# Three slots' low parts on GpSimd, and 4 products of zeros in place of 12

## The chip, the cores and the metric

The kernel runs on one core of one Trainium2 chip. The metric is the device time of one execution in microseconds, the median of three timed runs. One more execution was recorded by the hardware profiler, and all rows shown below are of that execution. TensorE is PE in the rows, VectorE is DVE, ScalarE is ACT, GpSimd is POOL and SyncE is SP.

## The reference

Two transformer blocks over 256 tokens of width 1024, all in float32. The first has two layers: latent attention (MLA), then sliding-window attention (SWA), each followed by an MLP of width 4096. The second has three branches (an RWKV recurrence, stick-breaking attention, attention to 256 memory tokens), gates over them and a convolutional feed-forward. Around the change the reference does this:

```
x = _layernorm(alpha * x + swa, ln_mix_g, ln_mix_b)      # third norm, "ln2" in the kernel
h = relu(x @ w_up); y = (h * h) @ w_down                  # "mlp1"
x = _layernorm(alpha * x + y, ln_mlp_g, ln_mlp_b)         # fourth norm, "ln3"
p = rms_norm(x, norm1_g) @ w_in                           # fifth norm, "rms1", then "rwkv"
...
kv = rms_norm(mem, mem_g) @ w_kv                          # "memka" and "memkb" make its keys
```

## The kernel before

**Products in three parts.** Each float32 operand is cut into a high part (rounded to the format fp32r) and a low part (the rest). A product is three matmuls: high by high, low by high, high by low.

**Weights in slots.** All weights come as one stream of slots of 128x1024 values (512 KB), in the order of the list STREAM, through a ring of four buffers (RING = 4). SP loads a slot into `raw`. ACT makes its high part `whi` (L1435) and raises the semaphore `cut_hi`. DVE then subtracts (`wlo` = `raw` - `whi`, L2047) and raises `cut_lo`. PE waits on `cut_lo` before it reads a slot. SP waits on `cut_lo` too: it loads slot n once the low part of slot n-4 is made. ACT makes the high part of slot n once PE has begun slot n-3. The call `cuts(stage, s)` on ACT and on DVE makes slot `SLOT[stage] + s + 3` (AHEAD = 3), so it stands some steps ahead of the slot's use. Where each call stands is written by hand in the program of each engine.

**The three slots of this change.** Slot A is the second of `mlp1`; its cut comes at the last share of the attention's output product. Slot B is the third of `memkb`; its cut comes behind the last hidden unit of `mlp1`. Slot C is the first of `rwkv`; its cut comes between the fourth norm and the fifth.

**Norms.** `residual` (L2070) is four DVE instructions over a quarter of the tokens' values each (128x512). A quarter waits for its accumulator bank `acc` to be full, reads the bank from PSUM and `x` from SBUF, and writes `res` and a sum. ACT squares each quarter (L1500), DVE works out mean and variance in small instructions (L2074 to L2089), ACT takes the root (L1505). For `ln2` DVE and ACT scale the quarters (L2097, L1516), PE transposes them (L764, in `feature_major`), ACT makes the high parts `xh` and DVE the low parts `xl`, and `chunk_pair` begins the next product. Ahead of `ln2` PE computes the chunk `memka`, ahead of `rms1` the three chunks `memkb` and then products of zeros. Between `ln3` and `rms1` DVE makes `x` in eight instructions (L2354, then L2359, each 128x512, each reading two tensors in SBUF), ACT squares it again, and DVE scales it (L2117). In `chunk_pair` PE waits for the low part of the second of two slots before its first product.

**GpSimd** does a few memsets and DMA issues, in program order. Ahead of the place of the change it issues the bias rows of `swa`, behind it the rows of the fourth norm's gain and bias (`affine_rows(3)`), which wait for DVE late in `mlp1`, and then two memsets that wait for the fifth norm's root.

Of the kernel before, what the change touches and what calls it, by code (L numbers as in the profile page):

```python
# [17 lines left out]
F32 = mybir.dt.float32  # L18
# [3 lines left out]
ALU = mybir.AluOpType  # L22
# [5 lines left out]
DC = D // P  # L28
# [5 lines left out]
FC = DFF // P  # L34
# [5 lines left out]
RING = 4  # L40
AHEAD = 3
# [5 lines left out]
SLOT = {}  # L47
# [120 lines left out]
SWA_SLOT = {key: n for n, key in enumerate(SWA_SLOTS)}  # L168
# [140 lines left out]
def build(nc, w, xt, x_tok, ln_rows, memt, mem_tok, consts_in, band_in, params_in, lora_in, gate2_in, relb_in, out):  # L309
    ctx = ExitStack()  # L310
    with ctx:
# [8 lines left out]
        raw = tensor(ctx, "raw", [P, RING, 1024])  # L320
        whi = tensor(ctx, "whi", [P, RING, 1024], F32R)
        wlo = tensor(ctx, "wlo", [P, RING, 1024], F32R)
# [130 lines left out]
        def of_tokens(name, width=2):  # L453
            first = {"mem_sum": 0, "mem_square": 2, "inverse": 4, "root": 8, "q_root": 10, "less_q_root": 12, "mem_least": 14, "large": 16, "rms_eps": 17, "lnx_eps": 18}[name]
            return cols[:, first:first + width]
# [98 lines left out]
        cut_hi = sem("cut_hi")  # L554
        cut_lo = sem("cut_lo")
# [3 lines left out]
        def sig(name):  # L559
            if name not in named:  # L560
                named[name] = sem(name)
            return named[name]
# [48 lines left out]
        @block.gpsimd  # L611
        def _(pool):
            nc.gpsimd.memset(zeros[:, :], 0.0).then_inc(sig("zeros_set"), 1)

            def affine_rows(n):

                if n:
                    pool.wait_ge(sig("affine_done"), n)
                else:
                    wait_drained(pool, ("mla", ("o", MLA_H - 1)))  # L620
                pool.dma_start(gb[:, :, :].rearrange("p a d -> p (a d)"), bass.AP(ln_rows.tensor, n * 2 * D, [[0, P], [1, 2 * D]]))\
                    .then_inc(sig("affine_loaded"), 16)

            nc.gpsimd.memset(of_tokens("large", 1), 3.0e38).then_inc(sig("large_set"), 1)
            nc.gpsimd.memset(of_tokens("rms_eps", 1), RMS_EPS).then_inc(sig("eps_set"), 1)
            nc.gpsimd.memset(of_tokens("lnx_eps", 1), LNX_EPS).then_inc(sig("eps_set"), 1)
            pool.dma_start(relb[:, :], relb_in).then_inc(sig("band_loaded"), 16)
            pool.dma_start(bandt, band_in).then_inc(sig("band_loaded"), 16)

            wait_drained(pool, ("brow", 0))  # L630
            pool.dma_start(scratch, brow).then_inc(sig("brow_stored"), 16)
            pool.wait_ge(sig("brow_stored"), 16)
            pool.dma_start(lora[:, :], lora_in).then_inc(sig("lora_loaded"), 16)
            pool.dma_start(gate2[:, :], gate2_in).then_inc(sig("lora_loaded"), 16)
            pool.wait_ge(sig("qr_ready"), 2)
            pool.dma_start(con[:, CCOL["blockones"]:], consts_in[:, CCOL["blockones"]:]).then_inc(sig("con2_loaded"), 16)

            def bias_rows(head, heads, loaded):


                pool.dma_start(bias[:, head % 8:head % 8 + heads, :], bass.AP(scratch.tensor, head * 384, [[1, P], [384, heads], [1, T]]))\
                    .then_inc(sig(loaded), 16)

            affine_rows(0)
            bias_rows(0, 8, "bias_loaded0")
            affine_rows(1)
            affine_rows(2)
            for first in (8, 12):
                for n in range(first - 8, first - 4):
                    wait_drained(pool, ("swa", ("s", n)))  # L650
                for half_ in (0, 4):
                    bias_rows(8 + (first - 8) // 2 + half_, 2, f"bias_loaded{first}")
            affine_rows(3)

            pool.wait_ge(sig("rstd"), 5)
            for j in range(3):
                wait_drained(pool, ("memkb", j))
            nc.gpsimd.memset(pb[:, :, 0:1], 0.0).then_inc(sig("pb_zero"), 1)
            nc.gpsimd.memset(cum[:, :, 0:1], 0.0).then_inc(sig("pb_zero"), 1)
            wait_drained(pool, ("mem", ("o", 3)))  # L660
            nc.gpsimd.memset(cg[:, :, 0:2], 0.0).then_inc(sig("cg_zero"), 1)
            nc.gpsimd.memset(cv[:, :, 0:2], 0.0).then_inc(sig("cg_zero"), 1)
# [3 lines left out]
        def _(pe):  # L666
# [85 lines left out]
            def feature_major(name, idle=0):  # L752


                n = SCALED[name]
                zero_products(open_result((name, 0)), idle)
                for d, t in ((0, 0), (0, 1), (1, 0), (1, 1)):
                    if (d, t) == (1, 0):
                        pe.wait_ge(sig("scaled_act"), n + 1)
                    else:  # L760
                        pe.wait_ge(sig("scaled_dve"), 3 * n + d + t + 1)
                    for i in ((0, 1, 2), (3, 4))[d]:
                        for c, dst in turned_chunks(name, i):
                            last = nc.tensor.transpose(dst[:, half(t)], rest[:, t, c * P:c * P + P], C("ident"))  # L764
                        if t == 1 and i < 4:
                            last.then_inc(sig("turned"), 1)
                        elif t == 1:
                            close_result(last, (name, 0))
# [104 lines left out]
            for p in range(4):  # L873
                bank = open_result(("k", p))
                for e in range(2):
                    for c in range(2):
                        s, tile = divmod(2 * (2 * p + e) + c, 8)
# [14 lines left out]
            for kind, n in MLA_PE:  # L892
# [10 lines left out]
                elif kind in "rn":  # L903
                    bank = open_result(key)
                    for e in range(2):
                        for k in range(3):
                            s, tile = divmod(MLA_TILE[(kind, n)] + 3 * e + k, 8)
# [127 lines left out]
            mlp("mlp1", "ln2")  # L1035
            for j in range(3):
                chunk("memkb", j, ("memkb", j), memh, meml)
            feature_major("rms1", 12)
            chunk_pair("rwkv", [("rwkv", 0), ("rwkv", 1)], "rms1")
            for j in range(2, 4):  # L1040
                chunk("rwkv", j, ("rwkv", j), xh, xl)
# [132 lines left out]
            for tc in range(2):  # L1174
# [98 lines left out]
                for c in range(4):  # L1273
                    for src, of in ((vtok[:, tc, :], rk), (sa, rb)):
                        for g, off in enumerate(HALVES):
                            h = 2 * c + g
# [98 lines left out]
            for r in range(24):  # L1375

                bank = open_result(("branch", r))
                n = SLOT["branch"] + r // 2
# [659 lines left out]
        def _(dve):  # L2038
# [10 lines left out]
            def cuts(stage, s, it=None, per=0):  # L2049
                cut(SLOT[stage] + s + AHEAD, it, per)  # L2050

            def fill_cut(i):

                cuts("sbqk", i)
# [59 lines left out]
            def rms_norm(name, g, ahead=None):  # L2114
                inverse(name, False)
                for t, d in ((0, 0), (1, 0), (1, 1)):
                    ts(tok(rest, t, d), tok(x, t, d), column("rstd", t), None, ALU.mult).then_inc(sig("scaled_dve"), 1)  # L2117
                if ahead:
                    ahead()
                for i in range(5):  # L2120
                    dve.wait_ge(sig("x_hi"), 5 * SCALED[name] + i + 1)
                    for c, src in turned_chunks(name, i):
                        ins = stt(xl[:, c, :], src, G(g, c), xh[:, c, :].bitcast(F32), ALU.mult, ALU.subtract)
                    if i < 4:
                        ins.then_inc(sig("x_low"), 1)
                    else:
                        drain(ins, (name, 0))
# [199 lines left out]
            for p, turn in enumerate(SWA_TURNS):  # L2327
                heads = (2 * p, 2 * p + 1) if p < 8 else ()
                if p in (0, 4, 6):
                    dve.wait_ge(sig(f"bias_loaded{2 * p}"), 32 if p else 16)  # L2330
                for h in heads:
                    g = SWA_ORDER[h]
                    negative_scores("swa", h, three, SWA_D ** -0.5, (bias[:, g % 8, P - 1::-1], bias[:, g % 8, ::-1]), nsink[:, g:g + 1])
                for kind, h in turn:
                    if kind == "q":
                        cuts("swaqo", SWA_SLOT[(kind, h)])
                for h in heads:
                    normalise("swa", h, three, True)
                for kind, h in shares_last(turn):
                    if kind == "o":  # L2340
                        key = ("swa", ("o", h))
                        dve.wait_ge(sig("oh_hi"), 8 + h + 1)
                        drain(minus(ol[:, h, :], work[RESULT[key] % 4][:, 0:T], oh[:, h, :]), key)
                    elif kind == "w":
                        cuts("swaqo", SWA_SLOT[(kind, h)])
            layer_norm("ln2", "swa", "ln_mix_g", "ln_mix_b", 8)
            cuts("memka", 0)
            mlp("mlp1", FC, 2)
            cuts("mlp1", 2 * FC - 1)
            residual("ln3", "mlp1")  # L2350
            dve.wait_ge(sig("affine_loaded"), 64)
            for t in range(2):
# [4 lines left out]
            for t in range(2):  # L2357
                for d in range(2):
                    stt(tok(x, t, d), tok(x, t, d), column("rstd", t), tok(gb, 1, d), ALU.mult, ALU.add).then_inc(sig("x_made"), 1)  # L2359
            cuts("memkb", 0)  # L2360
            rms_norm("rms1", "norm1", lambda: cuts("memkb", 1))
            cuts("memkb", 2)
            dve.wait_ge(sig("pb_zero"), 2)
            def by_halves(tile):
# [497 lines left out]
```

## Time and profile before

| | |
|---|---|
| median of 3 runs | 1086.45 us (1086.35 to 1087.44) |
| profiled execution | 1088.7 us, of which the span of its instructions is 1086.9 us |
| granted TensorE clock, mean | 0.998 |
| PE busy | 1065.5 us (98%) |
| DVE busy | 762.2 us (70%) |
| ACT busy | 642.5 us (59%) |
| POOL busy | 10.0 us (1%), 27 instructions |
| third norm | about 378 to 391 us from the span's start |
| fourth and fifth norm | about 566 to 586 us |

Busy shares are averages over the whole span. PE's records overlap, so a busy PE says little; what counts at a norm is where PE's next product waits. In a timeline each row gives the start, the duration, engine, line and operation, what is written and read, a count, and in brackets how long the engine had been idle before it and who released it. Where a row merges several instructions, its duration is that of the whole group.

### The profile page before, as it was taken

The numbers are of one execution on the slowest core, as the hardware profiler recorded it, in microseconds if no ns is written. First come the engines' busy times: TensorE is split into PE (matmuls) and PEld (weight loads), VectorE is DVE, ScalarE is ACT, GpSimd is POOL, SyncE is SP. The second block draws the span as 40 slices with busy tenths as digits, with TensorE's granted clock in tenths as the row PEclk, the third lists the DMA queues.
The fourth block names the chain that finished last, engine by engine and source line by source line (L and its number), as shares of the span: only waits on it lengthen the run. The fifth ranks groups of instructions, "written<-read, shape, count | busy, mean of one in ns | idle before, by whom it ended". The sixth has DMA issues, their size and how long they took to land.

```text
span 1086.9 us, 22249 instructions
## 1 busy us (share of the span) xinstructions
PE 1065.5 (98%) x8247; PEld 960.5 (88%) x8247; DVE 762.2 (70%) x1313; ACT 642.5 (59%) x1159; POOL 10.0 (1%) x27
## 2 busy tenths in 40 slices
PE   6999999999999999999999999999999999999998
PEld 5978999988887789988988988898899979999997
DVE  4877756557796775555677878646774968777776
ACT  4876654544676764444558874435567448666663
POOL 1000000000000000000000000000000000000000
PEclk9999999999999999999999999999999999999999
DMA  9545565566665346666663533122245655656562
GB/s 350 181 164 203 190 189 191 185 184 183 204 211 156 103 154 191 187 182 186 181 230 119 165 126 115 44 79 79 78 156 173 195 155 160 206 177 185 186 193 94
DMA packets 49170, 181.76 MB, mean 167 GB/s; under 512 B 5536, under 2 KB 5696, under 8 KB 48208
## 3 DMA queue, kind: packets, MB, share of 16 engines
q1 hardware_dynamic: 46512, 168.32, 49.1%
q0 software_dynamic: 1584, 7.63, 2.4%
q10 hardware_dynamic: 1008, 4.89, 1.2%
q8 instruction: 47, 0.77, 0.3%
q14 instruction: 19, 0.16, 0.0%
HBM read 179.74 MB, written 1.07 MB: 166 GB/s over the span
## 4 chain that ended last, share of the span: by engine, by line
PE 91%; DVE 4%; ACT 3%; issue 1%; DMA 1%; POOL 0%; DVEq 0%; ACTq 0%; POOLq 0%
PE acc L739 28%; PE work L686 13%; PE work L690 13%; PE work L689 13%; PE acc L686 4%; PE acc L689 3%; PE acc L690 3%; ACT whi L1435 1%; DVE wlo L2047 1%; PE work L724 1%; DMA qlat<-band_rows 1%; DVE res L2070 1%; PE work L810 1%; PE work L887 1%; PE work L714 1%
## 5 line engine op out<-in xcount | busy, mean ns | idle before, releaser
L2047 DVE TENSOR_TENSOR wlo<-raw,whi 128x1024 fp32r<-128x1024 f32 x319 | 388.9, 1223 | 143.5 <-ACT whi L1435 141.8
L1435 ACT ACTIVATE whi<-raw 128x1024 fp32r<-128x1024 f32 x319 | 335.9, 1056 | 120.2 <-PE acc L739 84.2
L686 PE MATMUL work<-xh,whi 128*128 128x256 f32 x1024 | 290.2, 283 | 0.6 <-ACT k_ L1776 0.2
L689 PE MATMUL work<-xl,whi 128*128 128x256 f32 x1024 | 289.2, 282 | 0.0
L690 PE MATMUL work<-xh,wlo 128*128 128x256 f32 x1024 | 289.1, 282 | 0.0
L686 PEld LDWEIGHTS work<-xh,whi 128*128 128x128 f32 x1024 | 194.5, 190 | 7.9 <-issue 2.1
L689 PEld LDWEIGHTS work<-xl,whi 128*128 128x128 f32 x1024 | 194.2, 190 | 3.5
L690 PEld LDWEIGHTS work<-xh,wlo 128*128 128x128 f32 x1024 | 194.8, 190 | 0.0
L739 PE MATMUL acc<-whi,hl 128*128 128x512 f32 x344 | 108.0, 395 | 0.0
L739 PE MATMUL acc<-wlo,hh 128*128 128x512 f32 x344 | 108.0, 395 | 0.0
L739 PE MATMUL acc<-whi,hh 128*128 128x512 f32 x344 | 108.0, 395 | 0.0
L686 PE MATMUL acc<-xh,whi 128*128 128x256 f32 x288 | 86.8, 301 | 0.0
L1669 ACT ACTIVATE ha<-work 128x256 f32<-128x256 f32 x64 | 24.6, 384 | 99.7 <-PE work L686 94.8
L689 PE MATMUL acc<-xl,whi 128*128 128x256 f32 x288 | 81.3, 282 | 0.0
L690 PE MATMUL acc<-xh,wlo 128*128 128x256 f32 x288 | 81.3, 282 | 0.0
L739 PEld LDWEIGHTS acc<-whi,hl 128*128 128x128 f32 x344 | 64.5, 188 | 15.8
L739 PEld LDWEIGHTS acc<-wlo,hh 128*128 128x128 f32 x344 | 64.5, 187 | 15.4
L739 PEld LDWEIGHTS acc<-whi,hh 128*128 128x128 f32 x344 | 59.5, 189 | 8.4
L2288 DVE TENSOR_TENSOR hb<-ha 128x256 f32<-128x256 f32 x64 | 27.2, 425 | 45.4 <-ACT ha L1669 45.4
L686 PEld LDWEIGHTS acc<-xh,whi 128*128 128x128 f32 x288 | 54.8, 190 | 3.3 <-issue 1.4
L689 PEld LDWEIGHTS acc<-xl,whi 128*128 128x128 f32 x288 | 54.9, 191 | 0.8 <-issue 0.7
L690 PEld LDWEIGHTS acc<-xh,wlo 128*128 128x128 f32 x288 | 54.8, 190 | 0.0
(456 smaller groups left out, 1635.5 us busy)
## 6 DMA issues: line engine op xcount, KB each, us to landing
raw<-weights SPq DMA_DIRECT2D x319, 512.0 KB, 3.6
gb<-ln_rows POOLq DMA_DIRECT2D x4, 1024.0 KB, 7.4
memraw<-mem_t ACTq DMA_DIRECT2D x1, 1024.0 KB, 15.4
x<-mem_tok ACTq DMA_DIRECT2D x1, 1024.0 KB, 18.5
x<-x_tok ACTq DMA_DIRECT2D x1, 1024.0 KB, 7.8
qlat<-bias_scratch POOLq DMA_DIRECT2D x1, 1024.0 KB, 9.8
qlat<-bias_scratch POOLq DMA_DIRECT2D x4, 256.0 KB, 4.2
out_tok<-res SPq DMA_DIRECT2D x4, 256.0 KB, 2.1
```

Of the source, the lines that this page charges most:

```text
L686: a = mm(dst, whi[:, n % RING, col], hi, start=start, stop=False, skip_group_check=shared)
L689: mm(dst, whi[:, n % RING, col], lo, start=False, stop=False, skip_group_check=shared)
L690: return mm(dst, wlo[:, n % RING, col], hi, start=False, stop=stop, skip_group_check=shared)
L714: a = mm(banks[j][:, 0:T], whi[:, (n + j) % RING, col], xh[:, k, :], start=k == 0, stop=False)
L724: last = mm(banks[j][:, 0:T], whi[:, (n + j) % RING, k * P:k * P + P], xl[:, k, :], start=False, stop=k == DC - 1)
L739: ins = mm(acc[2 * t + d][:, :], left[:, half(t)], right[:, n % RING, d * 512:d * 512 + 512], start=first and a == 0, stop=last and a == 2)
L810: last = mm(dst, src[:, half(t)], one.broadcast_to([P, heads, width // heads]), start=True, stop=True)
L887: last = nc.tensor.transpose(bank[:, b * P:b * P + P], probability_buffer(stage, h)[:, a * P:a * P + P], C("ident"))
L1435: act_fn(whi[:, n % RING, :], raw[:, n % RING, :], ACT.Copy).then_inc(cut_hi, 1)
L1669: act_fn(ha[:, f % 2, :], bank[:, 0:T], ACT.Relu).then_inc(sig("relu"), 1)
L2047: tt(wlo[:, n % RING, :], raw[:, n % RING, :], whi[:, n % RING, :].bitcast(F32), ALU.subtract).then_inc(cut_lo, 1)
L2288: tt(hb[:, f % 2, :], ha[:, f % 2, :], ha[:, f % 2, :], ALU.mult).then_inc(sig("h_squared"), 1)
```

## The change

Three low parts are no longer made by DVE but by GpSimd, with the same subtraction, in GpSimd's own program order. GpSimd waits for the slot before to have its low part and for the slot's own high part. DVE waits for GpSimd ahead of the slots that follow A and C, so that the counts of `cut_lo` stay in order. The products of zeros ahead of the fifth norm's transposes go from 12 to 4.

```diff
+            def low_part(n):
+
+                pool.wait_ge(cut_lo, n)
+                pool.wait_ge(cut_hi, n + 1)
+                nc.gpsimd.tensor_tensor(wlo[:, n % RING, :], raw[:, n % RING, :], whi[:, n % RING, :].bitcast(F32), ALU.subtract).then_inc(cut_lo, 1)
+
...
+            low_part(SLOT["swaqo"] + SWA_SLOT[("w", DC - 1)] + AHEAD)
             affine_rows(3)
+            low_part(SLOT["mlp1"] + 2 * FC - 1 + AHEAD)
+            low_part(SLOT["memkb"] + AHEAD)
...
-            feature_major("rms1", 12)
+            feature_major("rms1", 4)
...
+            def cuts_behind_pool(stage, s):
+
+                dve.wait_ge(cut_lo, SLOT[stage] + s + AHEAD)
+                cuts(stage, s)
+
...
-                    elif kind == "w":
+                    elif kind == "w" and h < DC - 1:
                         cuts("swaqo", SWA_SLOT[(kind, h)])
             layer_norm("ln2", "swa", "ln_mix_g", "ln_mix_b", 8)
-            cuts("memka", 0)
+            cuts_behind_pool("memka", 0)
             mlp("mlp1", FC, 2)
-            cuts("mlp1", 2 * FC - 1)
             residual("ln3", "mlp1")
...
-            cuts("memkb", 0)
-            rms_norm("rms1", "norm1", lambda: cuts("memkb", 1))
+            rms_norm("rms1", "norm1", lambda: cuts_behind_pool("memkb", 1))
             cuts("memkb", 2)
```

## Rows read from the trace of the kernel before

**Rows 1.** The page: shares of the chain that ended last, by engine.
```profile
PE 91%; DVE 4%; ACT 3%; issue 1%; DMA 1%; POOL 0%; DVEq 0%; ACTq 0%; POOLq 0%
```

**Rows 2.** Timelines of DVE, third norm: slot A's cut, first and last quarter, variance.
```profile
376.87 1.22 DVE L2047 TENSOR_TENSOR wlo<-raw,whi 128x1024 fp32r<-128x1024 f32 x1 [0.30 <-ACT whi L1435]
378.01 0.68 DVE L2070 SCALAR_TENSOR_TENSOR res<-x,acc 128x512 f32<-128x512 f32 x1
...
379.83 0.68 DVE L2070 SCALAR_TENSOR_TENSOR res<-x,acc 128x512 f32<-128x512 f32 x1
...
381.46 0.16 DVE L2088 TENSOR_TENSOR stat<-stat 128x2 f32<-128x2 f32 x1
```

**Rows 3.** Timeline of PE, third norm: last banks, transposes.
```profile
377.62 0.63 PE L739 MATMUL acc<-whi,ol 128*128 128x512 f32 x2
...
382.86 1.28 PE L764 MATMUL acc<-con,res 128*128 128x128 f32 x10 [1.77 <-DVE res L2097]
```

**Rows 4.** Timelines of PE and DVE ahead of the sixth norm, where DVE is not late.
```profile
889.42 0.63 PE L739 MATMUL acc<-whi,xl 128*128 128x512 f32 x2
...
889.85 2.69 DVE L2676 TENSOR_TENSOR x<-x,acc 128x512 f32<-128x512 f32 x4 [1.36 <-PE acc L739]
```

**Rows 5.** Timelines of ACT, third norm: table load, first and last square.
```profile
376.86 1.28 ACT L1485 ACT_TABLE_LOAD   x1
...
378.80 0.63 ACT L1500 ACTIVATE sqr<-res 128x512 f32<-128x512 f32 x1 [0.44 <-DVE res L2070]
...
380.65 0.61 ACT L1500 ACTIVATE sqr<-res 128x512 f32<-128x512 f32 x1
```

**Rows 6.** Timeline of DVE, fourth and fifth norm.
```profile
565.40 1.22 DVE L2047 TENSOR_TENSOR wlo<-raw,whi 128x1024 fp32r<-128x1024 f32 x1 [0.91 <-ACT whi L1435]
...
568.37 0.68 DVE L2070 SCALAR_TENSOR_TENSOR res<-x,acc 128x512 f32<-128x512 f32 x1
...
569.69 2.74 DVE L2354 SCALAR_TENSOR_TENSOR x<-res,stat,gb 128x512 f32<-128x512 f32 x4
...
575.94 1.22 DVE L2047 TENSOR_TENSOR wlo<-raw,whi 128x1024 fp32r<-128x1024 f32 x1
...
577.28 0.16 DVE L2088 TENSOR_TENSOR stat<-stat 128x2 f32<-128x2 f32 x1
...
579.10 1.22 DVE L2047 TENSOR_TENSOR wlo<-raw,whi 128x1024 fp32r<-128x1024 f32 x1
```

**Rows 7.** Timeline of ACT, fourth and fifth norm: two high parts, last square.
```profile
569.74 1.99 ACT L1435 ACTIVATE whi<-raw 128x1024 fp32r<-128x1024 f32 x2
...
576.06 0.63 ACT L1500 ACTIVATE sqr<-x 128x512 f32<-128x512 f32 x1
```

**Rows 8.** Timeline of PE, fourth and fifth norm.
```profile
566.15 0.63 PE L739 MATMUL acc<-whi,hl 128*128 128x512 f32 x2
566.62 0.28 PE L686 MATMUL work<-memh,whi 128*128 128x256 f32 x1
...
575.14 2.76 PE L750 MATMUL work<-zeros 128*128 128x512 bf16 x12
578.45 1.31 PE L764 MATMUL acc<-con,res 128*128 128x128 f32 x10 [0.55 <-DVE res L2117]
...
580.58 0.36 PE L714 MATMUL work<-xh,whi 128*128 128x256 f32 x1 [0.16 <-issue]
```

**Rows 9.** Timeline of POOL, whole span: two memsets.
```profile
0.74 0.20 POOL L613 MEMSET zeros<- 128x128 bf16 x1 [0.29 <-POOLq L2856]
...
579.35 0.11 POOL L659 MEMSET cum<- 128x8 f32 x1
```

**Rows 10.** The page: DMA issues of `raw` (count, size, median us to landing).
```profile
raw<-weights SPq DMA_DIRECT2D x319, 512.0 KB, 3.6
```

**Rows 11.** Timeline of PE at the start: first and last of 26 products.
```profile
10.19 1.46 PE L861 MATMUL work<-qlat,relb 32*16 32x384 f32 x2 [10.19 <-DMA qlat<-band_rows]
...
11.96 0.41 PE L689 MATMUL work<-xl,whi 128*128 128x256 f32 x1
...
17.29 0.41 PE L690 MATMUL work<-xh,wlo 128*128 128x256 f32 x1
```

## The prediction, made before the change was built

> **What bounds the kernel now.** I read the page's chain of work that ended last, then the waits of PE, then the timelines of each engine at the three norms. The chain runs through PE for 91% of the span [rows 1], so a microsecond taken off another engine counts only where PE waits for that engine. At the third norm the wait is plain: PE has idled 1.77 us when the transposes start at 382.86, released by DVE's scaling [rows 3]. At the fifth norm PE idles 0.55 us ahead of the transposes at 578.45, and it stood in 2.76 us of products of zeros just before [rows 8]; so for 578.45 - 575.14 = 3.3 us it had nothing of use to do. Before both waits DVE makes a low part of 1.22 us in the middle of the norm's chain: slot A at 376.87 [rows 2], slot B at 565.40 and slot C at 575.94 [rows 6]. The question is what each stands in front of.
>
> **Third norm, slot A.** Without the cut a quarter of the residual starts when its bank is full. How soon that can be is read ahead of the sixth norm: the last pair of matmuls of a half starts at 889.42 and DVE at 889.85, 0.43 us later [rows 4]. Here the second half's last pair starts at 377.62 [rows 3], so its quarters (the third and fourth) can start at 378.05 and, with the pitch of (379.83 - 378.01) / 3 = 0.61 us, at 378.66. The fourth started at 379.83 [rows 2]: DVE is 1.17 us earlier. But ACT is in between. It loads a function table at 376.86 for 1.28 us, and the first square at 378.80 shows an idle time of only 0.44 us [rows 5]: ACT is free at 378.36 whatever DVE does. Its squares have a pitch of (380.65 - 378.80) / 3 = 0.62 us, so the last one moves from 380.65 to 380.21. From the last square the chain is serial (variance, root, scaling, transposes). I take **0.40 us** of gain, 0.44 less a little for the step out of the table load. DVE's remaining 0.7 us goes into waiting for ACT.
>
> **Fourth norm, slot B.** The last pair starts at 566.15 [rows 8], so the fourth quarter can start at 566.15 + 0.43 + 0.61 = 567.19. It started at 568.37 [rows 6]: **1.18 us**. ACT is no limit: its squares follow, and its two high parts (569.74 [rows 7]) end more than 1 us before the root is wanted. The second of them needs PE to be in the second `memkb` chunk. The three chunks fill 566.62 to 575.14 [rows 8], 2.84 us each, so that is from 569.46 on, and it costs nothing. After the small instructions the eight two-tensor instructions that make `x` follow back to back, so all 1.18 us is kept.
>
> **Slot C.** The cut ran from 575.94, and the next thing DVE did on the chain was the variance at 577.28 [rows 6]. Without the cut this instruction waits for ACT's last square, which started at 576.06 [rows 7]. At the third norm it came 381.46 - 380.65 = 0.81 us after the last square [rows 2, 5], here that makes 576.87, a gain of **0.41 us**. The rest of the 1.22 us goes to the wait for ACT.
>
> **Zeros.** With 1.59 us gained, transposes can start at 578.45 - 1.59 = 576.86. Twelve products of zeros take 2.76 us and would end at 577.90, so they would have eaten 1.0 us of that. Four end at 575.14 + 4 x 0.23 = 576.06 and leave PE idle for 0.8 us. That part costs nothing and gains nothing beyond letting the 1.59 us through. What sets PE's first real product at 580.58 is the low part of the slot after C, at 579.10 for 1.22 us [rows 6, 8]; it hangs on the same DVE chain and moves with it.
>
> **What GpSimd's subtraction costs.** No row has one. From below: memsets take 0.11 us for 8 columns and 0.20 for 128 [rows 9], some 0.8 ns a column, so 1024 columns written once would be 0.9 us. From above, with two streams read and one written, each at that pace: 0.1 + 3 x 0.8 = 2.6 us. I take 2.6, since the subtraction does have three streams. The Trainium skill ("GPSIMD Engine Reference", section "Elementwise — side-by-side cycle accounting") gives 4497 ns for 2048 values of a two-input float32 instruction, which would be an estimate of 2.25 us here. No run here shows it.
>
> Slack, in times of before: A can start when ACT's high part is done, at about 376.9, and PE needs it only behind transposes that start at about 382.4, 5.5 us later. B starts at 565.45 and is wanted by PE's third `memkb` chunk at 575.14 - 2.84 = 572.3. C starts behind its high part, about 1.2 us earlier than 569.74 + 1.0, at 569.5, and is wanted by DVE at about 577.5. All three bear some 5 us. SP loads the slot four further on behind each low part: behind A and B those loads go out about 1.5 us later, behind C some 4 us earlier. A load lands in 3.6 us [rows 10] and its cut is three slots of PE work later, so none becomes late. Behind A, GpSimd's next entry is a DMA wanted near the end of `mlp1`; behind C come two memsets that wait for the fifth root in any case. DVE's two new waits are over before DVE gets there.
>
> **Sum.** 0.40 + 1.18 + 0.41 = 1.99, call it 2.0 us. The profiled execution would go from 1088.7 (span 1086.9) to 1086.7 (1084.9). It lay 2.25 us above the median of the runs, 1086.45; so the forecast for the median is **1084.4 us**, 0.19% less. The measurement can tell about 0.2% (2.2 us) from no change. The gain lies just inside that.
>
> **Rival 1: GpSimd and DVE get in each other's way at slot C.** GpSimd would read `raw` and `whi` from about 569.5 to 572.1. DVE then stands in the instructions of L2354 (moved to 568.5 to 571.2), which read two tensors in SBUF, and then in small ones and in L2359, which do so too. A and B run beside the residual, which reads one tensor in SBUF and one in PSUM. If DVE has to stand still for one whole GpSimd instruction, the chain loses between 0.9 and 2.6 us. At 2.6 the sum is -2.0 + 2.6 = +0.6 us, **1087.05 us**, slower than before; it turns from gain to loss where the stop is over 2.0 us. Nothing in the trace has GpSimd reading beside DVE, so nothing excludes it. The Trainium skill says just this ("SBUF — State Buffer", section "Who interferes with whom"): a VectorE instruction with two SBUF inputs and a GpSimd instruction that reads SBUF contend for a shared port, and the later one blocks until the first is done. With that page's rule and the 2.25 us above, the time would be 1086.7.
>
> **Rival 2: they share.** DVE is slowed, not stopped, while GpSimd reads. Half of rival 1's loss, 1.3 us: **1085.7 us**.
>
> **Rival 3: PE's clock falls ahead of `rwkv`.** After 10.19 us idle at the start, 26 products took (17.29 - 11.96) / 25 = 0.213 us each [rows 11]; in `memkb` 72 take (575.14 - 566.62) / 72 = 0.118. I read the first as the lower level, 1.2 GHz. Such a stretch costs 26 x 0.095 = 2.5 us and would give **1086.9 us**. It needs the shorter row of zeros to leave PE too quiet: from 576.06 to the first real product at 579.0 there would be only the transposes. Against it: at the third norm PE idled 1.77 us ahead of the transposes, with no zeros at all [rows 3], and the products there keep the fast pace. It decides against the change from 21 slow products on. It is likelier where rival 1 makes the idle time long (3.4 us).
>
> **Rival 4: GpSimd is much slower than thought.** From some 5.5 us an instruction, slot A is late for PE, and each further microsecond costs one. At 7 us it would be 1084.4 + 1.5 = **1085.9 us**. Nothing in the rows speaks for it.
>
> **How the numbers follow.** Forecast (no conflict) 0.45; rival 1 0.20; rival 2 0.18; rival 3 0.08; rival 4 0.04; something else 0.05. The range must reach rival 1: **1083.8 to 1087.1**; its low end is the forecast less 0.6 for the 0.4 of table load that ACT may give back and the scatter of the runs. Faster by over 0.2% (below 1084.28) takes somewhat under half of the forecast's chance and a little of the rest: 0.25. Slower by over 0.2% (above 1088.6) takes rivals 1 and 3 together or something unseen: 0.09. Within 0.2%: 0.66.
>
> **What would show it.** In the profile after, the third norm's first quarter starts about 376.65 and ACT's last square about 0.4 us earlier; at the fourth norm, measured from the last matmul on `acc`, the fourth quarter starts 1.04 us later instead of 2.22; DVE's four of L2354 still take 2.74 us (if 5, rival 1; if 3.5 to 4.5, rival 2). GpSimd's three subtractions take 2 to 3 us. PE's transposes start about 1.7 us after the last `memkb` product, and the first `rwkv` products keep 0.118 us each (0.213: rival 3). I am wrong if L2354 or the small instructions behind it stretch, or if ACT, not DVE, holds the chain at the fourth norm.

## The result

The changed kernel is slower: 1089.36 us median of 8 runs (1087.69 to 1092.31) against 1086.39 us of 8 (1086.15 to 1087.44), a ratio of 1.0024 with a 95% interval of 1.0015 to 1.0033. The forecast was 1084.4 us, in a range of 1083.8 to 1087.1.

The profiled execution took 1089.38 us with a span of 1087.6 us. Line numbers moved: in the kernel after, L2047 is L2056, L2070 is L2084, L2354 is L2367, L2117 is L2131, L739 is L748, L764 is L773 and L1500 is L1509.

First GpSimd's timeline of the kernel after, its three subtractions:

```profile
376.38 2.42 POOL L628 TENSOR_TENSOR wlo<-raw,whi 128x1024 fp32r<-128x1024 f32 x1 [39.44 <-ACT whi L1444]
...
564.52 2.42 POOL L628 TENSOR_TENSOR wlo<-raw,whi 128x1024 fp32r<-128x1024 f32 x1 [10.18 <-ACT whi L1444]
568.74 2.45 POOL L628 TENSOR_TENSOR wlo<-raw,whi 128x1024 fp32r<-128x1024 f32 x1 [1.80 <-ACT whi L1444]
```

They take 2.42 to 2.45 us, between the forecast's bounds of 0.9 and 2.6. Next the third norm after, timelines of PE, DVE and ACT:

```profile
377.02 0.63 PE L748 MATMUL acc<-whi,ol 128*128 128x512 f32 x2
...
381.85 1.28 PE L773 MATMUL acc<-con,res 128*128 128x128 f32 x10 [1.37 <-DVE res L2111]
```

```profile
376.05 0.69 DVE L2084 SCALAR_TENSOR_TENSOR res<-x,acc 128x512 f32<-128x512 f32 x1
...
378.06 0.68 DVE L2084 SCALAR_TENSOR_TENSOR res<-x,acc 128x512 f32<-128x512 f32 x1
...
380.45 0.16 DVE L2102 TENSOR_TENSOR stat<-stat 128x2 f32<-128x2 f32 x1 [0.45 <-ACT sqr L1509]
```

```profile
376.25 1.28 ACT L1494 ACT_TABLE_LOAD   x1
...
377.78 0.63 ACT L1509 ACTIVATE sqr<-res 128x512 f32<-128x512 f32 x1
...
379.64 0.61 ACT L1509 ACTIVATE sqr<-res 128x512 f32<-128x512 f32 x1
```

The fourth quarter starts 378.06 - 377.02 = 1.04 us after the last pair on `acc` (2.21 before [rows 2, 3]). The first square has no idle time in front of it any more: ACT is just out of the table load. The transposes start 4.83 us after that pair, 5.24 before [rows 3]: 0.41 us gained. GpSimd's first subtraction ran from 376.38 to 378.80 beside this residual, and the third quarter at 377.45 and the fourth at 378.06 still stand 0.61 us apart, as before.

Now the fourth and fifth norm after, timeline of DVE, and then the four instructions of L2367 by themselves (operation and count, then minimum, median and maximum in ns, first and last start):

```profile
564.18 0.69 DVE L2084 SCALAR_TENSOR_TENSOR res<-x,acc 128x512 f32<-128x512 f32 x1 [0.69 <-PE acc L748]
...
566.19 0.68 DVE L2084 SCALAR_TENSOR_TENSOR res<-x,acc 128x512 f32<-128x512 f32 x1
...
567.51 4.89 DVE L2367 SCALAR_TENSOR_TENSOR x<-res,stat,gb 128x512 f32<-128x512 f32 x4
...
573.26 2.74 DVE L2372 SCALAR_TENSOR_TENSOR x<-x,stat,gb 128x512 f32<-128x512 f32 x4 [0.27 <-ACT stat L1514]
...
576.85 0.16 DVE L2102 TENSOR_TENSOR stat<-stat 128x2 f32<-128x2 f32 x1 [0.56 <-ACT sqr L1509]
...
577.48 1.28 DVE L2131 TENSOR_SCALAR res<-x,stat 128x512 f32<-128x512 f32 x3 [0.27 <-ACT stat L1514]
578.67 1.22 DVE L2056 TENSOR_TENSOR wlo<-raw,whi 128x1024 fp32r<-128x1024 f32 x1
```

```profile
L2367 DVE SCALAR_TENSOR_TENSOR x<-res,stat,gb x4: 741/750/2893, 567.5 to 571.7; 128x512 f32<-128x512 f32 x4
```

The four take 4.89 us where they took 2.74 [rows 6]. Three are as before; one, the third, takes 2893 ns. It began at about 568.8, as GpSimd began slot C, and ended at 571.7, half a microsecond after GpSimd's end at 568.74 + 2.45 = 571.19. I call the 4.89 - 2.74 = 2.15 us that it adds the stop. The same for PE, timeline after:

```profile
565.14 0.63 PE L748 MATMUL acc<-whi,hl 128*128 128x512 f32 x2
...
574.13 1.04 PE L759 MATMUL work<-zeros 128*128 128x512 bf16 x4
578.02 1.80 PE L773 MATMUL acc<-con,res 128*128 128x128 f32 x10 [2.86 <-DVE res L2131]
...
580.75 0.56 PE L723 MATMUL work<-xh,whi 128*128 128x256 f32 x1
581.11 0.42 PE L726 MATMUL work<-xh,wlo 128*128 128x256 f32 x1
...
587.09 0.28 PE L695 MATMUL work<-xh,whi 128*128 128x256 f32 x1
```

PE idles 2.86 us ahead of the transposes, 0.55 before [rows 8]. The ten transposes take 1.80 us instead of 1.31. The windows of the kernel after show why (the third number from the end of each row is the granted clock, as a share of 2.4 GHz):

```profile
core 0: us, PE busy (x) PEld busy (x) DVE busy (x) ACT busy (x) POOL busy (x), PEclk, DMA share, GB/s
578.00:579.00 1.00, 0.98 (x8) 0.98 (x9) 1.00 (x3) 0.92 (x4) 0.11 (x2) 0.85 0.00 0
579.00:582.00 3.00, 3.00 (x16) 3.00 (x15) 2.88 (x7) 2.68 (x8) 0.04 (x1) 0.50 0.29 46
582.00:583.00 1.00, 1.00 (x10) 1.00 (x10) 1.00 (x4) 1.00 (x2) 0.00 (x0) 0.95 0.94 385
```

The granted clock is 0.50, the lower of its two levels (1.2 GHz), from shortly after the idle time until about 582. Products there start 0.21 us apart (581.33, then 581.54). That is the pace of the products at the start of the kernel before [rows 11], which the forecast read as the lower level; the clock column of before gives 1.00 there, from 10 to 18 us, so only the pace shows it.

Counted from the last pair on `acc`, the scalings start at 577.48 - 565.14 = 12.34 us where it was 11.76 (577.91, in the same timeline of before, less 566.15). That is 0.58 us late: -1.18 (slot B), +2.15 (the stop), and -0.39 is left for slot C. DVE's variance shows the same for C: it starts 576.85 - 576.03 = 0.82 us after ACT's last square, 577.28 - 576.06 = 1.22 before [rows 6, 7]. The third chunk of `rwkv` starts 587.09 - 565.14 = 21.95 us after the pair; in the timeline of before its first row is at 586.35, 20.20 us after. So 1.75 us are lost; 0.58 of them are there when the scalings start, and the other 1.17 come behind that, where the clock is low. I put these down to the clock.

The two profiled spans differ by only 0.7 us, because this execution was 1.01 us ahead when it came to the fourth norm: 0.41 is slot A's gain, the other 0.60 it had before it reached anything that was changed. And the profiled execution of before has a loss of its own. Its windows for PE in the recurrence (start and end, length, busy time and instructions of PE, granted clock, DMA share, GB/s):

```profile
728.00:730.00 2.00, 2.00 (x21) 1.00 0.00 0
730.00:732.00 2.00, 2.00 (x15) 0.75 0.00 0
732.00:734.00 2.00, 2.00 (x11) 0.50 0.00 0
734.00:736.00 2.00, 2.00 (x26) 0.90 0.46 139
```

The clock falls here too, behind 32 small products (128x32) of 4.03 us in all from 727.88, without idle time. The changed kernel's profile has this fall as well (0.57 in the windows from 732 to 736), so it has two. The mean granted clock of each run tells such falls apart: of 35 runs of the kernel before on the chip of the first experiments, 22 had a clock of 0.999 or 1.0 (median 1086.43 us, span 1084.6) and 13 had 0.997 or 0.998 (median 1088.03, span 1086.2). Of the 8 runs of the changed kernel one had 1.0 (span 1084.8) and seven had 0.995 to 0.997 (span 1087.0 to 1089.5). So with no fall the change is worth about nothing, by this one run, and nearly every run of it has a fall. Runs "without a fall" are below those at 0.999 or 1.0. The profiles give a scale: those with one fall of the length seen here have a mean of 0.998 (before, and the sixth and ninth experiment), those with two 0.997 and 0.996 (after, and the fifth experiment).

### The profile page after: what moved, and what is told of

Read it like the earlier page. It is cut to its first block, busy times and chain, and to the rows that moved or that the text cites. A ratio compares the mean times of both kernels' runs of the same rounds, so it can differ in the third digit from the quotient of the medians.

```text
span 1087.6 us, 22240 instructions
## 1 busy us (share of the span) xinstructions
PE 1064.3 (98%) x8239; PEld 960.5 (88%) x8239; DVE 761.3 (70%) x1310; ACT 642.7 (59%) x1159; POOL 17.4 (2%) x30
## 3 DMA queue, kind: packets, MB, share of 16 engines
q10 hardware_dynamic: 1008, 4.89, 1.1%
## 4 chain that ended last, share of the span: by engine, by line
PE 89%; DVE 5%; ACT 3%; DMA 2%; issue 1%; DVEq 0%; ACTq 0%; SPq 0%
PE acc L748 28%; PE work L695 12%; PE work L699 12%; PE work L698 12%; PE acc L695 4%; PE acc L699 3%; PE acc L698 3%; ACT whi L1444 1%; PE work L733 1%; DMA sqr<-x_t 1%; DVE wlo L2056 1%; DMA raw<-weights 1%; PE work L819 1%; PE work L726 1%; PE work L723 1%
## 5 line engine op out<-in xcount | busy, mean ns | idle before, releaser
L2056 DVE TENSOR_TENSOR wlo<-raw,whi 128x1024 fp32r<-128x1024 f32 x316 | 385.3, 1223 | 143.1 <-ACT whi L1444 141.5
L748 PE MATMUL acc<-whi,hl 128*128 128x512 f32 x344 | 108.1, 395 | 0.0
L748 PE MATMUL acc<-wlo,hh 128*128 128x512 f32 x344 | 108.0, 395 | 0.0
L748 PE MATMUL acc<-whi,hh 128*128 128x512 f32 x344 | 108.0, 395 | 0.0
L748 PEld LDWEIGHTS acc<-whi,hl 128*128 128x128 f32 x344 | 64.5, 188 | 15.7
L748 PEld LDWEIGHTS acc<-wlo,hh 128*128 128x128 f32 x344 | 64.5, 187 | 15.3
L748 PEld LDWEIGHTS acc<-whi,hh 128*128 128x128 f32 x344 | 59.6, 189 | 8.3
```

The costliest lines, as they stand in the source:

```text
L748: ins = mm(acc[2 * t + d][:, :], left[:, half(t)], right[:, n % RING, d * 512:d * 512 + 512], start=first and a == 0, stop=last and a == 2)
L2056: tt(wlo[:, n % RING, :], raw[:, n % RING, :], whi[:, n % RING, :].bitcast(F32), ALU.subtract).then_inc(cut_lo, 1)
```

## The experiments

**Twelve zeros again, the rest of the change kept.**

```diff
-            feature_major("rms1", 4)
+            feature_major("rms1", 12)
```

> The changed kernel with 12 products of zeros again. Theory (port and clock): VectorE is stopped at slot C for 2.15 us by GpSimd's subtraction, and the rest of the loss is TensorE's clock falling in the gap that 4 products leave. Then L2367's four still take 4.9 us, no product of the fifth norm runs at the slow pace, and the time is that of the kernel before plus 2.15 - 2.0 = 0.15 us, 1086.3 to 1086.9. Rival (late work, not zeros): the clock falls because the transposes come late, whatever stands ahead of them; then it stays near 1089.3 with slow products after 578.

1086.98 us, ratio 1.0002 (0.9993 to 1.0010). Seven of 11 runs have no fall, with a median of 1086.89 (span 1085.1); the other four are all at 0.998, one fall each by the scale above, about the share that the kernel before has. PE's timeline, then DVE's instructions of L2367:

```profile
573.98 2.76 PE L759 MATMUL work<-zeros 128*128 128x512 bf16 x12
577.88 1.31 PE L773 MATMUL acc<-con,res 128*128 128x128 f32 x10 [1.13 <-DVE res L2131]
```

```profile
L2367 DVE SCALAR_TENSOR_TENSOR x<-res,stat,gb x4: 741/748/2896, 567.4 to 571.5; 128x512 f32<-128x512 f32 x4
```

DVE's stop is there to within 3 ns, the transposes are fast again, and the kernel is level with the one before. So most of the measured loss hangs on the eight zeros taken away, and the stop has eaten the whole of the gain. Runs without a fall are still 0.46 us slower than before.

**Slot C back on DVE, four zeros.**

```diff
-            low_part(SLOT["memkb"] + AHEAD)
...
-            rms_norm("rms1", "norm1", lambda: cuts_behind_pool("memkb", 1))
+            cuts_behind_pool("memkb", 0)
+            rms_norm("rms1", "norm1", lambda: cuts("memkb", 1))
```

> The changed kernel with slot C's low part on VectorE as before; A and B on GpSimd, 4 products of zeros. Port theory: L2367's four take 2.74 us again, transposes start 1.2 us after the zeros end, the gain of A and B (0.4 + 1.18 = 1.6 us) comes through, 1084.8 us, if the clock holds over a gap of 1.2 us plus the transposes. If the clock falls even so, up to 2.5 us more, 1085 to 1087.3. Rival (GpSimd's work slows VectorE wherever it runs): no more than half of 1.6 us is gained and the residual's pitch is over 0.61 us.

1085.41 us, ratio 0.9988 (0.9979 to 0.9996). Without a fall 1085.05 (8 of 12 runs; span 1083.05, 1.55 less than before). DVE's and PE's timelines:

```profile
567.13 2.74 DVE L2366 SCALAR_TENSOR_TENSOR x<-res,stat,gb 128x512 f32<-128x512 f32 x4
```

```profile
573.75 1.04 PE L758 MATMUL work<-zeros 128*128 128x512 bf16 x4
575.89 1.31 PE L772 MATMUL acc<-con,res 128*128 128x128 f32 x10 [1.10 <-DVE res L2130]
```

The stop is gone, and by the spans A and B bring what the forecast gave them, 1.6 us (1.37 by the times, 1085.05 against 1086.43). The rival that GpSimd slows DVE wherever it runs falls. With 1.10 us of idle time ahead of the transposes this profile has no fall at all, and 4 of 12 runs have one, about the share of the kernel before: four zeros did no harm that these runs show.

**The kernel before, with four zeros.**

```diff
-            feature_major("rms1", 12)
+            feature_major("rms1", 4)
```

> The kernel before with 4 products of zeros and nothing else. Clock theory: TensorE is idle for 2.4 us ahead of the transposes at 578.45 instead of 0.55 us; if that is enough for the clock to fall, products after it run at 0.213 us and the time is 1 to 3 us over before, 1087.4 to 1089.4, with a wide scatter. If the fall needs the longer gap that GpSimd makes (2.9 us), it is 1086.4, as before.

1089.41 us, ratio 1.0017 (1.0008 to 1.0026). Only 2 of 11 runs have no fall, against 22 of 35 of the kernel before on the same chip; the other nine are at 0.996 to 0.998. PE idles 2.27 us ahead of the transposes in its profile, which happens to be one of the two without a fall. So taking the zeros away makes falls likely with no work on GpSimd; no profile of this kernel shows where the clock falls.

**A and B on GpSimd, C on DVE, nine zeros.** The kernel of the second experiment with `feature_major("rms1", 9)`.

> Slot C's low part on VectorE, A and B on GpSimd, 9 products of zeros, which end at about the time when the transposes are ready. Both theories: 1.6 us less than before, 1084.8 us, with little scatter. Rival (GpSimd slows VectorE anywhere): 1085.6 or more.

1086.17 us, ratio 0.9989 (0.9980 to 0.9998). Without a fall 1085.18 (span 1083.4, 1.2 less than before), but only in 5 of 11 runs. Nine zeros filled the gap and the transposes started with no idle time, and still six runs had a fall. The profile is of a run without one, so whether the six fell in the recurrence is not known.

**Only slot C on GpSimd, twelve zeros.** The two helper functions of the change come with it.

```diff
             affine_rows(3)
+            low_part(SLOT["memkb"] + AHEAD)
...
-            cuts("memkb", 0)
-            rms_norm("rms1", "norm1", lambda: cuts("memkb", 1))
+            rms_norm("rms1", "norm1", lambda: cuts_behind_pool("memkb", 1))
```

> The kernel before with only slot C's low part on GpSimd, 12 products of zeros. Port theory: the four of L2354 take 4.9 us instead of 2.74, so the chain is 2.15 us longer and 0.41 us shorter: runs without a clock fall at 1086.4 + 1.75 = 1088.1 us, and some more with one. Rival (the stop comes from A and B having delayed something in the ring): L2354 takes 2.74 us and the time is 1086.0.

1089.76 us, ratio 1.0021 (1.0013 to 1.0030). Without a fall 1088.49 against 1086.65 for the kernel before on this chip: +1.84 us, where 1.75 was expected. Three of 12 runs have no fall. Timelines of POOL, DVE and PE:

```profile
570.52 2.44 POOL L628 TENSOR_TENSOR wlo<-raw,whi 128x1024 fp32r<-128x1024 f32 x1 [15.60 <-ACT whi L1442]
```

```profile
569.28 4.89 DVE L2366 SCALAR_TENSOR_TENSOR x<-res,stat,gb 128x512 f32<-128x512 f32 x4
```

```profile
579.81 0.50 PE L771 MATMUL acc<-con,res 128*128 128x128 f32 x2 [2.32 <-DVE res L2129]
```

The same 4.89 us, so the stop needs neither A nor B. The clock falls even behind twelve zeros, when the stop leaves 2.32 us of idle time: the granted clock is 0.50 in the window 581 to 583. This profile has the fall in the recurrence too, 0.50 in the window 734 to 736.

**A and B on GpSimd, C on DVE, eleven zeros.** As the kernel with nine, with `feature_major("rms1", 11)`.

> A and B on GpSimd, C on VectorE, 11 products of zeros. In the run with 9 the transposes began right behind the zeros and the first product waited 0.4 us for the slot behind C, so two more zeros (0.46 us) should cost 0.0 to 0.1 us. Runs without a clock fall at 1085.0 to 1085.2 us. If more zeros keep the clock up more often, the median is lower than with 9 (1086.17); if the falls of that kernel are those late in the recurrence, as in the profile of before, there is no difference.

1085.22 us, ratio 0.9979 (0.9970 to 0.9988), the lowest ratio here. Part of that is chance: on this chip 12 of 23 runs of the kernel before had a fall, and its median, 1087.75, is one of them. Eight of 11 runs have no fall (median 1085.09, 1.56 less than the 1086.65 of before on this chip). The two added zeros cost nothing that shows: 1.56 gained against 1.25 with nine zeros, each against the kernel before on its own chip. That falls are rarer than with nine zeros (3 of 11 against 6 of 11) is too few runs to be sure of. The profile is of one of the three: the transposes start with no idle time, the clock is 1.00 from 576 to 582, and it falls in the recurrence, 0.50 in the window 730 to 732.

**GpSimd writes only.** The kernel with nine zeros, and at slot C's moment a memset of 2048 columns of an unused tile.

```diff
+            pool.wait_ge(cut_lo, SLOT["memkb"] + AHEAD)
+            pool.wait_ge(cut_hi, SLOT["memkb"] + AHEAD + 1)
+            nc.gpsimd.memset(flat(oh).bitcast(F32), 0.0).then_inc(sig("idle_done"), 1)
```

> Slot C's low part on VectorE; in its place GpSimd sets 2048 columns of an unused tile to zero, released at the same moment. It only writes. If the stop comes from GpSimd's reads against VectorE's second input, the four two-tensor instructions take 2.74 us as without it. If any GpSimd instruction stops them, they take 2.74 us plus the memset, about 1.7 us.

Timelines of POOL and DVE:

```profile
568.50 1.81 POOL L664 MEMSET oh<- 128x2048 f32 x1 [1.79 <-ACT whi L1446]
```

```profile
567.30 2.74 DVE L2369 SCALAR_TENSOR_TENSOR x<-res,stat,gb 128x512 f32<-128x512 f32 x4
```

No stop at all. The one time, 1089.33 us, has a long fall in the recurrence, at a clock of 0.50 from 730 to 738, so it says nothing on the memset.

**GpSimd reads one tensor.** The same place and the same two waits, a copy of 2048 columns between two unused tiles.

```diff
+            nc.gpsimd.tensor_copy(flat(ol)[:, 0:2048], flat(oh)[:, 0:2048].bitcast(F32)).then_inc(sig("idle_done"), 1)
```

> As the run with the memset, but GpSimd copies 2048 columns between two unused tiles: one tensor read, one written. If reads are what stops VectorE, the four two-tensor instructions take 2.74 us plus nearly the whole copy (some 1.7 us or more). If it takes two streams read by GpSimd to stop it, 2.74 us.

```profile
568.51 1.95 POOL L664 CAST ol<-oh 128x2048 fp32r<-128x2048 f32 x1 [1.80 <-ACT whi L1446]
```

```profile
L2369 DVE SCALAR_TENSOR_TENSOR x<-res,stat,gb x4: 741/748/2393, 567.3 to 570.9; 128x512 f32<-128x512 f32 x4
```

One of the four takes 2393 ns instead of 748, 1.65 us more: reading one tensor is enough. The stop is 0.3 us shorter than GpSimd's instruction (1.95), as it was for the subtraction (2.15 against 2.45). The tiles are ones that DVE does not use at that time, so the stop is not about `raw` and `whi`.

**GpSimd beside DVE's scalings.** The kernel with nine zeros, and a subtraction on unused tiles behind `pool.wait_ge(sig("rstd"), 5)`. The scalings that the expectation calls L2130 are L2131 in this build.

```diff
+            nc.gpsimd.tensor_tensor(flat(ol)[:, 0:1024], flat(oh)[:, 0:1024].bitcast(F32), flat(oh)[:, 1024:2048].bitcast(F32), ALU.subtract).then_inc(sig("idle_done"), 1)
```

> A and B on GpSimd, C on VectorE, 9 products of zeros, and one more GpSimd subtraction of 1024 columns on unused tiles, released by the fifth norm's root, so that it runs beside VectorE's three scalings L2130 (one tensor in SBUF read, 1.28 us for the three) and the low part behind them (two tensors, 1.22 us). If only a second tensor in SBUF makes VectorE stand still, the scalings take 1.28 us and the low part behind them ends only after GpSimd (2.42 us from the root), some 1.2 us late. If scalings of one tensor use the shared port too (their 512 columns in 0.40 us a piece hint at two columns at once), either they or GpSimd's instruction are stretched: scalings at 2.4 us more, or a GpSimd span of 2.42 + 1.2 us.

```profile
576.01 2.35 POOL L664 TENSOR_TENSOR ol<-oh 128x1024 fp32r<-128x1024 f32 x1 [8.84 <-ACT stat L1514]
```

```profile
L2131 DVE TENSOR_SCALAR res<-x,stat x3: 468/475/2757, 576.0 to 579.0; 128x512 f32<-128x512 f32 x3
```

One of the three scalings takes 2757 ns instead of 475, though it reads one tensor in SBUF. So it isn't only a second tensor that makes DVE stand still. It is the first of the three, which begins at 575.97 in DVE's timeline, 0.04 us ahead of GpSimd; as the starts of GpSimd's instructions are rough in a profile, this doesn't tell which of the two came first. PE idles 2.29 us ahead of the transposes here, and the clock falls once more at the norm: 0.50 in the window 579 to 582, and 1.00 throughout the recurrence's windows from 724 to 738.

The profiles side by side, by PE's idle time ahead of the fifth norm's transposes: 2.86, 2.32 and 2.29 us with a fall there (after, fifth and ninth experiment); 2.27, 1.67 (the copy), 1.13, 1.10, 0.55 us and none at all without one. Each is a single execution.

## Why the prediction was wrong

**Slot A: right.** 0.40 us forecast, 0.41 measured, and by the step named: ACT's table load sets the first square.

**Slot B: right.** The fourth quarter came 1.04 us after the last pair on `acc`, as forecast. Where no clock fall comes in between, the three kernels with A and B alone are 1.37, 1.25 and 1.56 us faster than before (1.55, 1.2 and 1.55 by the spans), against 1.58 forecast.

**GpSimd's subtraction: right.** 2.42 us against 2.6 taken and 2.25 estimated from the Trainium skill ("GPSIMD Engine Reference", section "Elementwise — side-by-side cycle accounting"). None of the three kept PE waiting for its low part in the rows after.

**Slot C: the step that failed.** The sum costed GpSimd's work beside L2354 at nothing and gave that 0.45. One DVE instruction was held until GpSimd had ended, 2.15 us longer than without, and that is more than the 2.0 us of the whole forecast gain. The cut's removal itself brought its 0.39 us (0.41 forecast). Rival 1 had the place and the mechanism, and its bounds of 0.9 to 2.6 us hold the measured stop. It was seen and given 0.20. Here the page that it names (the Trainium skill, "SBUF — State Buffer", section "Who interferes with whom") agrees with the runs: two tensors in SBUF on DVE against a reading GpSimd instruction stop DVE (4.89 us for 2.74), and a writing one does not (2.74). The scaling form is stopped too (2757 ns for 475). The forecast had no row against that rule; it should have carried it.

**Zeros: the other step that failed.** "That part costs nothing" held only for idle times near the forecast's 0.8 us (1.10 in the second experiment, whose runs show no harm). The stop made it 2.86 us, and the clock fell: 1.17 us in this execution. The text had the link ("likelier where rival 1 makes the idle time long") but priced the two rivals apart, and took the kernel before as if it had no falls. Four zeros without any work on GpSimd already move the median by 2.9 us (1086.49 to 1089.41). The size per fall was taken too high: 1.17 us at the norm in this execution and 1.60 between the two groups of runs of before, against 2.5. That the changed kernel nevertheless loses some 2.5 us to the clock is because it has two: from the last pair ahead of the fourth norm to the last pair ahead of the sixth its profile takes 326.22 us (565.14 to 891.36), that of the first experiment, with no fall, 323.71 (564.99 to 888.70). The second fall was in no part of the forecast.

**The sum as it came out.** Without a fall: -0.41 - 1.18 - 0.39 + 2.15 = +0.17 us; measured +0.5 with twelve zeros (span 1085.1 against 1084.6). The profiles of the first and the third experiment, both without a fall, are 0.4 us apart (1084.9 and 1084.5); from the last pair ahead of the third norm to the last pair ahead of the sixth they are 0.25 apart (376.88 to 888.70 and 376.82 to 888.39). The rest lies outside the stretch that was changed, and its cause was not settled. What is left of the 3.0 us between the medians I put down to clock falls: seven of eight runs of the changed kernel have a mean clock of 0.995 to 0.997, and by its time of 1086.39 the median run of the kernel before has no fall.

**Still open.** Which of the falls in the timed runs lie at the fifth norm and which in the recurrence: only profiled executions show the place, and the changed kernel's shows one at each. Why a gap of 2.29 us had a fall and one of 2.27 had none is open too; no run varied the idle time by itself. Whether a fall at the norm makes the later one likelier was not tried: the profiles after and of the fifth experiment have both, that of the ninth only the one at the norm. Nor was GpSimd's work on C at a moment where DVE reads one tensor in SBUF and one in PSUM, since ACT's high part of C comes after the residual.

## What to carry to other kernels

Work moved to GpSimd was free here beside VectorE instructions with one tensor in SBUF and one in PSUM, and not beside those with two in SBUF or beside scalings from SBUF to SBUF. Before moving it, write down for its whole span what VectorE reads and writes and where, and price every clash at nearly the whole GpSimd instruction. A few products of zeros can be worth more than the time they take (here 2.76 - 1.04 = 1.7 us for eight, against 2.9 us of the median): shorten them only against the idle time that the kernel really has afterwards. Where runs of one kernel fall into groups by mean TensorE clock, compare within a group first, then count how often each kernel is in which.

## What the runs showed of the hardware

- DVE's residual, with one tensor in SBUF and one in PSUM, ran beside a GpSimd subtraction with its pitch of 0.61 us unchanged (377.45 to 378.06, inside 376.38 to 378.80).
- The stopped DVE instructions ended 0.4 to 0.5 us after GpSimd's (571.7 against 571.19, and 575.97 + 2.76 = 578.73 against 578.36 in the ninth experiment). Back-to-back DVE instructions did not keep GpSimd out: it started at 568.74, 0.14 us after the high part of slot C was done at 568.60, and the DVE instruction recorded from 568.8 was held.
- Scalings from SBUF to SBUF (0.475 us for 512 columns) are stopped as well, 2757 ns, in one execution.
- The kernel before falls to the lower clock in about a third to a half of its runs (13 of 35, 12 of 23), 1.6 us between the medians of the two groups on either chip. In its profile the fall came behind small products and not behind idle time.
